# Query and key norms from an exponential of a logarithm and a Newton step, with another order of the first query tiles

## Chip, cores and metric

The kernel runs on one core of a Trainium2 chip. The metric is the device time of one execution in microseconds, the median over several runs. The profile is one further execution, taken by the hardware profiler, with times from the span's start.

## What is computed

One step of a hybrid decoder layer on a prompt of 1024 positions and 8 sample tokens: a recurrent branch (RG-LRU), three groups of dilated window attention with 8 heads of width 64 each, a gated merge and a SwiGLU feed-forward block. The change touches the normalisation of queries and keys alone:

```python
def rmsnorm(x, g):
    xf = x.astype(jnp.float32)
    y = xf * lax.rsqrt(jnp.mean(xf * xf, axis=-1, keepdims=True) + EPS)
    return (y * g.astype(jnp.float32)).astype(x.dtype)

q = rmsnorm(q.reshape(B, T, N_ATT_HEADS, HEAD_DIM), q_gain)
k = rmsnorm(k.reshape(B, T, N_ATT_HEADS, HEAD_DIM), k_gain)
```

## The kernel before, in words

The activations lie transposed: channels on the 128 partitions, 1032 positions along the row. Every projection runs through one list of weights (`stream`, lines 159 to 173), as units of 128 output channels (`unit`, lines 461 to 475). A unit is three parts of 344 columns; each part is 24 products of TensorE: 8 blocks of the inner dimension times three, because each float32 factor is split into a high and a low float32r half. SP loads the raw weights (line 329), GpSimd splits them by a cast (line 448) and a subtraction (line 450) as soon as the unit two places ahead has set the slot free, and two PSUM slots of three banks (`ups`) take the units in turn.

The stage here is `qk`: 24 units, i from 0 to 11, slot j = 0 and 1. Tile (i, j) is number 2i + j: the first 12 tiles are queries, the last 12 keys, each with two heads. What happens to a tile:

- ScalarE, `evac` (lines 988 to 997): copies the unit out of PSUM to `tmp(j)`, squares it to `tmp(2 + j)`, and rounds the square to a high half `sq_parts[0]`. The same two halves serve all tiles, so the third step waits until the sums of the tile before are done.
- VectorE, `square_low` (line 1270): the low half `sq_parts[1]`.
- TensorE, `stats` (lines 553 to 560): four products with a matrix of ones per head put the sum of squares, spread over the partitions of its head, in `aux` (two PSUM banks). They wait for the low half and until the tile before has been read out of `aux`. Their place is written out by hand: the sums of one tile stand between the second and the third part of the next unit (`qk`, lines 562 to 566); the first tiles have an order of their own (lines 570 to 583).
- ScalarE, `root` (line 1006): the square root of the mean plus epsilon, from `aux` to `tmp(4 + j)`.
- VectorE, `normed_qk` (lines 1332 to 1338): the reciprocal in place (line 1335), then the tile times gain times reciprocal to `tmp(6 + j)` (line 1337). This sets `tmp(j)` free for the next copy.
- ScalarE's queue, `store` (line 1001): the tile to DRAM, from where the attention loads it again.

Each engine runs its instructions in program order. VectorE's order in the loop is `normed_qk(i, 0)`, `square_low(i, 1)`, `normed_qk(i, 1)`, `square_low(i + 1, 0)`; ScalarE's is `root(i - 1, 1)`, `evac(i, 0)`, `store`, `root(i, 0)`, `evac(i, 1)`, `store`. Ahead of the loop stands the end of the recurrent branch: VectorE finishes its last block (`recur`, lines 1272 to 1290, with the low half of tile (0, 0) between its steps), while TensorE already works on units (0, 0), (0, 1) and (1, 0). Behind it stands the first pair of attention heads (`pair`, lines 591 to 653): 24 products of the next projection, the sums of the last tile, further products, the transposes of the values (line 614), the scores (line 625). SP's loads for it (lines 391 to 403) take the buffers of the stage over: the values go to `tmp(2)`, the bias to the row of `sq_parts[0]`.

A list of semaphores carries all this: `qsh_done` and `qsl_done` (halves of the square), `st_done` (sums), `rt_done` (root), `qn_done` (normed tile), `qn_stored` (stored). `z_done` counts the blocks of the recurrent branch after line 1286, `lru_done` those after line 1289.

Of the kernel before, what the change touches and what calls it, by code (L numbers as in the profile page):

```python
# [23 lines left out]
ALU = mybir.AluOpType  # L24
ACT = mybir.ActivationFunctionType
# [3 lines left out]
P = 128  # L29
D = 1024  # L30
SEQ = 1024
# [4 lines left out]
KT = D // P  # L36
HD = 64
# [7 lines left out]
EPS = 1e-6  # L45
# [47 lines left out]
def build(nc, A, O):  # L93

    with ExitStack() as ctx:
# [12 lines left out]
        big1 = sb("big1", [P, 2, KT, NT], F32R)  # L108
# [35 lines left out]
        def tmp(n):  # L144

            return x1[:, n, :]
# [33 lines left out]
        def two(name):  # L180

            return [sem(f"{name}{j}") for j in range(2)]
# [23 lines left out]
        out_done, lru_done = sem("out_done"), sem("lru_done")  # L206

        qsq_done, st_done, rt_done, qn_done = two("qsq_done"), two("st_done"), two("rt_done"), two("qn_done")
        qsh_done, qsl_done = two("qsh_done"), two("qsl_done")
        qn_stored = two("qn_stored")  # L210
        sqc_done = sem("sqc_done")
# [110 lines left out]
        def _(sp):  # L322
            for name, iters, nk, src, f0, f1, step, k0 in stream:
# [67 lines left out]
                if name == "att0":  # L391
                    first = 1
                    weights(0, 0)
                    weights(0, 1)
                    for n in range(4):
                        sp.wait_ge(v_stored[n], 16)
                    sp.wait_ge(qn_stored[0], 16 * 8)
                    query_loads(0, 0)
                    sp.wait_ge(qsl_done[0], 12)
                    value_load(0, 0)  # L400
                    sp.wait_ge(bt_fill, 16)
                    sp.wait_ge(st_done[1], 13)
                    bias_load(0, 0)
# [56 lines left out]
        def _(pe):  # L460
# [92 lines left out]
            def stats(j, i):  # L553

                pe.wait_ge(qsl_done[j], i + 1)
                pe.wait_ge(rt_done[1 - j], i + 1)
                for c in range(2):
                    for a in range(2):
                        ins = nc.tensor.matmul(aux[:, c, :], bones_r[:], sq_parts[a][:, c * 512:(c + 1) * 512], start=(a == 0), stop=(a == 1))  # L559
                ins.then_inc(st_done[j], 1)  # L560
# [5 lines left out]
                    unit("qk", i, j, big1, parts=(2,))  # L566

            pe.sem_inc(rt_done[1], 1)
            pe.sem_inc(st_done[1], 1)
            for c in range(2):  # L570
                unit("qk", 0, 0, big1, parts=(c,))
# [4 lines left out]
            unit("qk", 1, 0, big1, parts=(0,))  # L576
            stats(0, 0)
            unit("qk", 1, 0, big1, parts=(1, 2))
            unit("qk", 1, 1, big1, parts=(0,))
            stats(1, 0)  # L580
            unit("qk", 1, 1, big1, parts=(1,))
            stats(0, 1)
            unit("qk", 1, 1, big1, parts=(2,))
            with pe.Fori(2, 12) as i:
# [5 lines left out]
            for g in range(NG):  # L590
                def pair(i, first, marks):
# [14 lines left out]
                    if first:  # L606
                        stats(1, 11)
                        pieces(8, marks[0])
                        pe.wait_ge(ps_free[1], T0["att0"] + 1)
                        pe.wait_ge(rt_done[1], 13)  # L610
                    pe.wait_ge(v_ld, i * 16 + 16 * (4 * g + 1))
                    pe.wait_ge(pt_ev, i * 4 + (16 * g + 1))
                    for b in range(8):
# [214 lines left out]
        def _(act):  # L828
# [174 lines left out]
            def root(i, j):  # L1003
                act.wait_ge(st_done[j], i + (1 + j))
                act.wait_ge(qn_done[j], i + 1)
                nc.scalar.activation(tmp(4 + j)[:, 0:SEQ], aux[:].rearrange("p b n -> p (b n)"), ACT.Sqrt, scale=1.0 / HD, bias=epst[:])\  # L1006
                    .then_inc(rt_done[j], 1)

            act.wait_ge(u_done, KT + 1)
            evac(0, 0)  # L1010
            act.wait_ge(lru_done, KT)
            act.dma_start(O["lru_out"], sout[:]).then_inc(out_done, 16)
            act.dma_start(O["state_out"], stc[:]).then_inc(out_done, 16)
            root(0, 0)
            evac(0, 1)
            with act.Fori(1, 12) as i:
                root(i - 1, 1)
                evac(i, 0)
# [177 lines left out]
        def _(dve):  # L1196
# [111 lines left out]
            normed(7)  # L1308
            normed_low(6)
            normed_low(7)  # L1310
            nc.vector.tensor_copy(bones_r[:], bones[:])
            for c in range(2):
                nc.vector.tensor_copy(gqk[:, 6 * c:6 * c + 6], gq2[:, c:c + 1].broadcast_to([P, 6]))
            step.step(nc.vector.tensor_scalar(bmrg[:], bmrg[:], 0.5, None, ALU.mult))
            dve.wait_ge(unit_done[1], T0["lru"] + 2)
            nc.vector.tensor_tensor(chunks(GE), ups_v[1], chunks(rinv), ALU.mult).then_inc(ps_free[1], 1)
# [13 lines left out]


            def normed_qk(i, j):
                rms_t = tmp(4 + j)[:, 0:SEQ]
                dve.wait_ge(rt_done[j], i + (1 + j))
                step.step(nc.vector.reciprocal(rms_t, rms_t))  # L1335
                dve.wait_ge(qn_stored[j], i * 16 + 16)
                nc.vector.scalar_tensor_tensor(tmp(6 + j)[:, 0:SEQ], tmp(j)[:, 0:SEQ], gqk[:, ds(i, 1)],
                                               rms_t, ALU.mult, ALU.mult).then_inc(qn_done[j], 1)

            with dve.Fori(0, 11) as i:  # L1340
                step.loop(i, 2)
                normed_qk(i, 0)
                square_low(i, 1)
                normed_qk(i, 1)
                square_low(i + 1, 0)
            step.end(11)
            step.loop(11, 2, 11)
            normed_qk(11, 0)
            square_low(11, 1)
            normed_qk(11, 1)  # L1350
# [40 lines left out]
            def s_norm():  # L1391
# [4 lines left out]
                step.step(nc.vector.reciprocal(rms, rms))  # L1396
                for c in range(2):
                    own = sqkv[:, 12 * c:12 * c + 12, :].rearrange("p f b -> p (f b)")
                    step.step(nc.vector.scalar_tensor_tensor(own, own, gqk[:, 6 * c:6 * c + 1], rms[:, 96 * c:96 * c + 96], ALU.mult, ALU.mult))
                dve.sem_inc(sq_normed, 1)  # L1400

            def s_build():
# [268 lines left out]
```

## Time and profile before

| What | Value |
|---|---|
| median of 3 runs | 2072.24 us (2071.32 to 2073.37) |
| the profiled execution | 2071.17 us |
| its span, first to last instruction | 2069.4 us |
| mean granted clock of TensorE | 0.993 |
| busy: TensorE, VectorE, ScalarE, GpSimd | 97%, 44%, 25%, 27% of the span |
| VectorE's reciprocals of line 1335 | 24, 157.3 us |

The span is the profiled execution without what lies before its first and after its last instruction. Engines are named in the rows by PE (TensorE's products; PEld its weight loads), DVE (VectorE), ACT (ScalarE), POOL (GpSimd) and SP; a queue that issues transfers has a q behind its engine. In a timeline a row is a start in us, a length in us, the engine, the source line, the operation, the tile written and those read, and how many instructions are merged; in brackets stands how long the engine was idle before it, and what ended that.

### The profile page before, as it was taken

What the parts mean: (1) busy time and instruction counts of PE and PEld (TensorE: products, weight loads), DVE (VectorE), ACT (ScalarE), POOL (GpSimd) and SP (SyncE); (2) the same over time, 40 slices, a digit from 0 to 9 for tenths busy, and PEclk for the clock granted to TensorE, in tenths of its full rate; (3) what the DMA queues carried; (4) which work ended last, traced back from release to release, by engine and by line L of the source; (5) the groups of instructions that cost most, each with busy time, mean ns of one, the idle gap of its engine ahead of it and who ended that gap; (6) DMA issues with size and microseconds to landing.
All of it is one profiled execution on the core that took longest, in us unless ns stands there. A gap on an engine that the chain in (4) does not pass through costs nothing.

```text
span 2069.4 us, 32282 instructions
## 1 busy us (share of the span) xinstructions
PE 2014.0 (97%) x12884; PEld 1952.3 (94%) x12884; DVE 905.9 (44%) x919; ACT 509.3 (25%) x726; POOL 552.1 (27%) x325
## 2 busy tenths in 40 slices
PE   7999998999989999999989899999999999999999
PEld 7999997999979999999978899999999999999999
DVE  6666677777762332222266553433311233212331
ACT  5366653333333433333311111201000000000000
POOL 2323332222211111111122143323323232323322
PEclk9999999999999999999999999999999999999999
DMA  5211111222223323334286361111111111111112
GB/s 200 97 44 43 43 46 61 93 90 81 101 97 135 116 97 136 114 111 149 87 307 236 125 239 51 44 48 51 41 51 41 51 42 49 51 41 51 41 59 84
DMA packets 71595, 188.45 MB, mean 91 GB/s; under 512 B 9313, under 2 KB 28796, under 8 KB 70780
## 3 DMA queue, kind: packets, MB, share of 16 engines
q1 hardware_dynamic: 41456, 136.97, 19.5%
q10 hardware_dynamic: 30092, 50.81, 6.7%
q8 instruction: 34, 0.56, 0.1%
q14 instruction: 13, 0.11, 0.0%
HBM read 145.09 MB, written 45.81 MB: 92 GB/s over the span
## 4 chain that ended last, share of the span: by engine, by line
PE 89%; DVE 6%; ACT 1%; issue 1%; DMA 1%; POOL 0%; ACTq 0%; SPq 0%; DVEq 0%; POOLq 0%
PE ups L472 64%; PE ups L600 13%; PE ups L625 3%; PE ups L650 3%; PE aux L637 2%; DVE x L1335 1%; PE aux L538 1%; PE aux L559 1%; PE ups L486 1%; PE aux L614 0%; DVE x L1489 0%; DVE x L1259 0%; DMA x<-o_s 0%; DVE x L1280 0%; ACT x L1076 0%
## 5 line engine op out<-in xcount | busy, mean ns | idle before, releaser
L472 PE MATMUL ups<-big,wsp 128*128 128x344 f32 x9216 | 1477.3, 321 | 9.1 <-POOL wsp L450 6.6
L472 PEld LDWEIGHTS ups<-big,wsp 128*128 128x128 f32 x9216 | 1459.4, 189 | 24.0 <-issue 16.9
L448 POOL CAST wsp<-wraw 128x1024 fp32r<-128x1024 f32 (+2 forms) x160 | 167.8, 1049 | 1485.0 <-issue 724.0
L450 POOL TENSOR_TENSOR wsp<-wraw,wsp 128x1024 fp32r<-128x1024 f32 (+2 forms) x160 | 384.0, 2400 | 12.8
L600 PE MATMUL ups<-big,wsp 128*128 128x344 f32 x1728 | 291.8, 324 | 0.0
L600 PEld LDWEIGHTS ups<-big,wsp 128*128 128x128 f32 x1728 | 272.7, 189 | 5.3 <-issue 5.2
L1335 DVE RECIPROCAL x<-x 128x1024 f32<-128x1024 f32 x24 | 157.3, 6553 | 74.4 <-ACT x L1006 74.4
L1372 DVE SCALAR_TENSOR_TENSOR x<-ups,ext 128x256 f32<-128x256 f32 (+1 forms) x96 | 48.0, 542 | 235.4 <-PE aux L637 147.4
L1181 ACT ACTIVATE ext<-ext 128x1032 f32<-128x1032 f32 x22 | 23.6, 1071 | 482.5 <-DVE ext L1589 482.4
L1591 DVE TENSOR_TENSOR ext<-ups,ext 128x1032 f32<-128x1032 f32 x22 | 27.1, 1233 | 215.4 <-PE ups L472 215.4
L1605 DVE TENSOR_TENSOR x<-ups,x 128x1032 f32 x24 | 29.6, 1233 | 203.6 <-PE ups L472 203.6
L1076 ACT ACTIVATE x<-x,ext 128x128 f32<-128x128 f32 (+1 forms) x192 | 71.2, 442 | 58.8 <-DVE ext L1380 58.4
L1594 DVE TENSOR_TENSOR ext<-ext 128x1032 f32<-128x1032 f32 x22 | 71.3, 3241 | 4.8 <-DVE ext L1591 4.8
L1589 DVE TENSOR_TENSOR ext<-ups,ext 128x1032 f32<-128x1032 f32 x22 | 27.1, 1234 | 105.3 <-PE ups L472 104.9
L625 PE MATMUL ups<-ext 64*128 64x128 f32 (+1 forms) x384 | 67.1, 476 | 4.7 <-DVEq L1357 4.7
L650 PE MATMUL ups<-x 128*128 128x65 f32 x560 | 67.8, 270 | 0.0
L650 PEld LDWEIGHTS ups<-x 128*128 128x128 f32 x560 | 66.8, 192 | 0.0
L1006 ACT ACTIVATE x<-aux,epst 128x1024 f32<-128x1024 f32 x24 | 26.8, 1117 | 132.5 <-PE aux L559 122.9
L625 PEld LDWEIGHTS ups<-ext 64*128 64x128 f32 x384 | 43.5, 281 | 14.6 <-issue 13.1
L1385 DVE COPY x<-ups 128x260 f32<-128x260 f32 x48 | 20.4, 425 | 81.4 <-PE ups L650 81.4
L1066 ACT ACTIVATE x<-aux 128x768 f32<-128x768 f32 (+1 forms) x32 | 28.6, 895 | 83.6 <-PE ups L650 67.5
L1378 DVE TENSOR_REDUCE x<-x 128x2 f32<-128x256 f32 (+1 forms) x96 | 47.6, 538 | 1.6
(190 smaller groups left out, 1147.9 us busy)
## 6 DMA issues: line engine op xcount, KB each, us to landing
wraw<-w_in SPq DMA_DIRECT2D x52, 512.0 KB, 3.4
wraw<-w_ffn_in SPq DMA_DIRECT2D x44, 512.0 KB, 3.2
out_qkv<-x ACTq DMA_DIRECT2D x28, 512.0 KB, 2.7
ext<-out_qkv SPq DMA_DIRECT2D x24, 512.0 KB, 4.3
x<-x_T SPq DMA_DIRECT2D x16, 516.0 KB, 8.2
x<-gate_s SPq DMA_DIRECT2D x16, 516.0 KB, 4.1
wraw<-w_merge SPq DMA_DIRECT2D x16, 512.0 KB, 4.9
wraw<-w_ffn_out SPq DMA_DIRECT2D x16, 512.0 KB, 3.5
```

Of the source, the lines that this page charges most:

```text
L448: nc.gpsimd.tensor_copy(hi, raw).then_inc(w_hi, 1)
L450: nc.gpsimd.tensor_tensor(lo, raw, hi.bitcast(F32), ALU.subtract).then_inc(w_split[slot], 1)
L472: ins = nc.tensor.matmul(ups[:, slot, c, 0:CH], wsp[:, slot, w, k, :], src[:, a, k, c * CH:(c + 1) * CH], start=(k == 0 and w + a == 0), s ...
L600: ins = nc.tensor.matmul(ups[:, 0, c, 0:CH], wsp[:, slot, w, k, :], big1[:, a2, k, c * CH:(c + 1) * CH], start=(k == 0 and w + a2 == 0), s ...
L625: ins = nc.tensor.matmul(s_bank[:, hh, 256 * m + 256 - P * nk:256 * m + 256], toks(QT, g, b)[hr], toks(KTT, g, b, nk)[hr], start=True, sto ...
L637: ins = nc.tensor.transpose(pt_bank[:, hh, c:c + P], SB[:, hh, c:c + P], ident[:])
L650: ins = nc.tensor.matmul(o_bank[:, at:at + HD + 1], PTS[:, hh, c:c + P], VTOK[:, b + 1 - nk + k, hh, :], start=(k == 0), stop=(k == nk - 1))
L1076: ins = nc.scalar.activation(SB[:, hh, cols], SB[:, hh, cols], ACT.Exp, bias=NM[:, 2 * m + hh:2 * m + hh + 1])
L1335: step.step(nc.vector.reciprocal(rms_t, rms_t))
L1372: ins = nc.vector.scalar_tensor_tensor(SB[:, :, cols], s_bank[:, :, cols], SCALE, BT[:, :, 0:P * nk][:, :, ::-1], ALU.mult, ALU.add)
L1378: ins = nc.vector.tensor_reduce(OT[:, 2 * n + m, :, HD + 1], SB[:, :, cols], AX_X, ALU.max)
L1594: step.step(nc.vector.tensor_tensor(ext[:, 1, 0:NT], ext[:, 0, 0:NT], ext[:, 1, 0:NT], ALU.mult))
```

## The change

ScalarE's root becomes two operations: the logarithm of the sum of squares plus epsilon, and the exponential of minus half of it, an estimate y of the reciprocal root. VectorE's reciprocal becomes a Newton step of three products: t = (sum + epsilon) y, t = t y, t = (t - 3) y, which with a gain of minus one half is the corrected value. The mean's 1/64 goes into the matrix of ones. The first product reads `aux` again, so `aux` is set free after it (a new semaphore `nt_done` takes the place of `rt_done` in TensorE's waits). The products use `tmp(2 + j)`, so SP's first load of values waits until tile (11, 0) is normed. At the stage's start ScalarE copies tile (0, 1) before the first root and issues two small output transfers after it; VectorE takes the low halves of (0, 1) and (1, 0) ahead of the tiles they stood behind; TensorE takes the sums of (0, 1) and (1, 0) at other places.

```diff
@@ -206 +206 @@
         qsq_done, st_done, rt_done, qn_done = two("qsq_done"), two("st_done"), two("rt_done"), two("qn_done")
+        lg_done, nt_done = two("lg_done"), two("nt_done")
@@ -396 +397 @@
                         sp.wait_ge(v_stored[n], 16)
                     sp.wait_ge(qn_stored[0], 16 * 8)
                     query_loads(0, 0)
-                    sp.wait_ge(qsl_done[0], 12)
+                    sp.wait_ge(qn_done[0], 13)
                     value_load(0, 0)
                     sp.wait_ge(bt_fill, 16)
                     sp.wait_ge(st_done[1], 13)
@@ -553 +554 @@
             def stats(j, i):
 
                 pe.wait_ge(qsl_done[j], i + 1)
-                pe.wait_ge(rt_done[1 - j], i + 1)
+                pe.wait_ge(nt_done[1 - j], i + 1)
                 for c in range(2):
                     for a in range(2):
                         ins = nc.tensor.matmul(aux[:, c, :], bones_r[:], sq_parts[a][:, c * 512:(c + 1) * 512], start=(a == 0), stop=(a == 1))
@@ -566 +567 @@
                     unit("qk", i, j, big1, parts=(2,))
 
             pe.sem_inc(rt_done[1], 1)
+            pe.sem_inc(nt_done[1], 1)
             pe.sem_inc(st_done[1], 1)
             for c in range(2):
                 unit("qk", 0, 0, big1, parts=(c,))
@@ -576 +578 @@
             unit("qk", 1, 0, big1, parts=(0,))
             stats(0, 0)
             unit("qk", 1, 0, big1, parts=(1, 2))
-            unit("qk", 1, 1, big1, parts=(0,))
             stats(1, 0)
-            unit("qk", 1, 1, big1, parts=(1,))
+            unit("qk", 1, 1, big1, parts=(0, 1))
             stats(0, 1)
             unit("qk", 1, 1, big1, parts=(2,))
             with pe.Fori(2, 12) as i:
@@ -607 +608 @@
                         stats(1, 11)
                         pieces(8, marks[0])
                         pe.wait_ge(ps_free[1], T0["att0"] + 1)
-                        pe.wait_ge(rt_done[1], 13)
+                        pe.wait_ge(nt_done[1], 13)
                     pe.wait_ge(v_ld, i * 16 + 16 * (4 * g + 1))
                     pe.wait_ge(pt_ev, i * 4 + (16 * g + 1))
                     for b in range(8):
@@ -1003 +1004 @@
             def root(i, j):
                 act.wait_ge(st_done[j], i + (1 + j))
                 act.wait_ge(qn_done[j], i + 1)
-                nc.scalar.activation(tmp(4 + j)[:, 0:SEQ], aux[:].rearrange("p b n -> p (b n)"), ACT.Sqrt, scale=1.0 / HD, bias=epst[:])\
+                nc.scalar.activation(tmp(4 + j)[:, 0:SEQ], aux[:].rearrange("p b n -> p (b n)"), ACT.Ln, bias=epst[:]).then_inc(lg_done[j], 1)
+                act.wait_ge(lg_done[j], i + 1)
+                nc.scalar.activation(tmp(4 + j)[:, 0:SEQ], tmp(4 + j)[:, 0:SEQ], ACT.Exp, scale=-0.5)\
                     .then_inc(rt_done[j], 1)
 
             act.wait_ge(u_done, KT + 1)
             evac(0, 0)
+            act.wait_ge(z_done, KT + 1)
+            evac(0, 1)
             act.wait_ge(lru_done, KT)
+            root(0, 0)
             act.dma_start(O["lru_out"], sout[:]).then_inc(out_done, 16)
             act.dma_start(O["state_out"], stc[:]).then_inc(out_done, 16)
-            root(0, 0)
-            evac(0, 1)
             with act.Fori(1, 12) as i:
                 root(i - 1, 1)
                 evac(i, 0)
@@ -1308 +1312 @@
             normed(7)
             normed_low(6)
             normed_low(7)
-            nc.vector.tensor_copy(bones_r[:], bones[:])
+            nc.vector.tensor_scalar(bones_r[:], bones[:], 1.0 / HD, None, ALU.mult)
             for c in range(2):
-                nc.vector.tensor_copy(gqk[:, 6 * c:6 * c + 6], gq2[:, c:c + 1].broadcast_to([P, 6]))
+                nc.vector.tensor_scalar(gqk[:, 6 * c:6 * c + 6], gq2[:, c:c + 1].broadcast_to([P, 6]), -0.5, None, ALU.mult)
             step.step(nc.vector.tensor_scalar(bmrg[:], bmrg[:], 0.5, None, ALU.mult))
             dve.wait_ge(unit_done[1], T0["lru"] + 2)
             nc.vector.tensor_tensor(chunks(GE), ups_v[1], chunks(rinv), ALU.mult).then_inc(ps_free[1], 1)
@@ -1330 +1334 @@
 
 
             def normed_qk(i, j):
-                rms_t = tmp(4 + j)[:, 0:SEQ]
+                y, t = tmp(4 + j)[:, 0:SEQ], tmp(2 + j)[:, 0:SEQ]
                 dve.wait_ge(rt_done[j], i + (1 + j))
-                step.step(nc.vector.reciprocal(rms_t, rms_t))
+                step.step(nc.vector.scalar_tensor_tensor(t, aux[:].rearrange("p b n -> p (b n)"), EPS, y, ALU.add, ALU.mult))
+                dve.sem_inc(nt_done[j], 1)
+                step.step(nc.vector.tensor_tensor(t, t, y, ALU.mult))
+                step.step(nc.vector.scalar_tensor_tensor(t, t, -3.0, y, ALU.add, ALU.mult))
                 dve.wait_ge(qn_stored[j], i * 16 + 16)
                 nc.vector.scalar_tensor_tensor(tmp(6 + j)[:, 0:SEQ], tmp(j)[:, 0:SEQ], gqk[:, ds(i, 1)],
-                                               rms_t, ALU.mult, ALU.mult).then_inc(qn_done[j], 1)
-
-            with dve.Fori(0, 11) as i:
-                step.loop(i, 2)
+                                               t, ALU.mult, ALU.mult).then_inc(qn_done[j], 1)
+
+            square_low(0, 1)
+            normed_qk(0, 0)
+            square_low(1, 0)
+            normed_qk(0, 1)
+            with dve.Fori(1, 11) as i:
+                step.loop(i, 6, 1)
                 normed_qk(i, 0)
                 square_low(i, 1)
                 normed_qk(i, 1)
                 square_low(i + 1, 0)
-            step.end(11)
-            step.loop(11, 2, 11)
+            step.end(10)
+            step.loop(11, 6, 11)
             normed_qk(11, 0)
             square_low(11, 1)
             normed_qk(11, 1)
@@ -1396 +1407 @@
                 step.step(nc.vector.reciprocal(rms, rms))
                 for c in range(2):
                     own = sqkv[:, 12 * c:12 * c + 12, :].rearrange("p f b -> p (f b)")
-                    step.step(nc.vector.scalar_tensor_tensor(own, own, gqk[:, 6 * c:6 * c + 1], rms[:, 96 * c:96 * c + 96], ALU.mult, ALU.mult))
+                    step.step(nc.vector.scalar_tensor_tensor(own, own, gq2[:, c:c + 1], rms[:, 96 * c:96 * c + 96], ALU.mult, ALU.mult))
                 dve.sem_inc(sq_normed, 1)
 
             def s_build():
```

## Rows read from the trace of the kernel before

**Rows 1.** The page, busy time: us, share of the span, instructions.

```profile
PE 2014.0 (97%) x12884; PEld 1952.3 (94%) x12884; DVE 905.9 (44%) x919; ACT 509.3 (25%) x726; POOL 552.1 (27%) x325
```

**Rows 2.** Busy time by stage: stretch, length, engines, then granted clock.

```profile
core 0: us, PE busy (x) PEld busy (x) DVE busy (x) ACT busy (x) POOL busy (x), PEclk, DMA share, GB/s
255.00:342.40 87.40, 77.92 (x462) 75.01 (x461) 62.11 (x43) 42.23 (x47) 23.53 (x12) 0.96 0.15 52
342.40:575.34 232.94, 232.94 (x1446) 229.55 (x1446) 170.50 (x57) 83.12 (x95) 65.47 (x38) 1.00 0.25 88
```

**Rows 3.** TensorE's timeline, 300 to 345 us.

```profile
302.04 11.49 PE L472 MATMUL ups<-big,wsp 128*128 128x344 f32 x72
316.54 1.20 PE L559 MATMUL aux<-ext_r,bones_r 128*128 128x512 f32 x4 [3.01 <-DVE ext_r L1270]
...
327.98 2.07 PE L559 MATMUL aux<-ext_r,bones_r 128*128 128x512 f32 x4 [6.48 <-DVE ext_r L1270]
...
342.40 1.09 PE L559 MATMUL aux<-ext_r,bones_r 128*128 128x512 f32 x4
```

**Rows 4.** Timeline of all engines in the loop, 425 to 442 us.

```profile
428.21 1.09 PE L559 MATMUL aux<-ext_r,bones_r 128*128 128x512 f32 x4
...
429.35 1.12 ACT L1006 ACTIVATE x<-aux,epst 128x1024 f32<-128x1024 f32 x1 [5.16 <-PE aux L559]
430.49 6.55 DVE L1335 RECIPROCAL x<-x 128x1024 f32<-128x1024 f32 x1 [3.25 <-ACT x L1006]
433.12 1.03 ACT L991 ACTIVATE x<-ups 128x1032 f32<-128x1032 f32 x1 [2.66 <-PE ups L472]
433.25 1.04 POOL L448 CAST wsp<-wraw 128x1024 fp32r<-128x1024 f32 x1 [8.72 <-issue]
...
434.37 2.40 POOL L450 TENSOR_TENSOR wsp<-wraw,wsp 128x1024 fp32r<-128x1024 f32 x1
...
437.27 1.28 DVE L1337 SCALAR_TENSOR_TENSOR x<-x,gqk 128x1024 f32<-128x1024 f32 x1 [0.23 <-DVE x L1335]
438.48 1.22 DVE L1270 TENSOR_TENSOR ext_r<-x,ext_r 128x1024 fp32r<-128x1024 f32 x1
```

**Rows 5.** Timeline of all engines ahead of the loop, 297 to 300 us.

```profile
297.66 2.01 POOL L448 CAST wsp<-wraw 128x1024 fp32r<-128x1024 f32 x1 [7.80 <-issue]
298.69 2.07 DVE L1286 TENSOR_TENSOR x<-x 128x1032 f32<-128x1032 f32 x1
299.75 3.26 POOL L450 TENSOR_TENSOR wsp<-wraw,wsp 128x1024 fp32r<-128x1024 f32 x1
```

**Rows 6.** Two lines of the feed-forward block: shortest, median, longest in ns.

```profile
L1594 DVE TENSOR_TENSOR ext<-ext x22: 2515/3276/3281, 1340.8 to 1998.1; 128x1032 f32<-128x1032 f32 x22
...
L1591 DVE TENSOR_TENSOR ext<-ups,ext x22: 1233/1233/1234, 1339.4 to 1996.7; 128x1032 f32<-128x1032 f32 x22
```

**Rows 7.** ScalarE's timeline: table loads before and in the stage.

```profile
2.14 1.28 ACT L852 ACT_TABLE_LOAD   x1 [2.14 <-issue]
...
30.44 0.21 ACT L869 ACTIVATE sqkv<-sqkv 128x8 f32<-128x8 f32 x1 [1.30 <-issue]
30.67 1.28 ACT L871 ACT_TABLE_LOAD   x1
...
288.90 1.28 ACT L949 ACT_TABLE_LOAD   x1
...
292.24 1.07 ACT L949 ACTIVATE x<-x 128x1032 f32<-128x1032 f32 x1 [2.06 <-DVE x L1275]
```

**Rows 8.** Timeline of all engines, 303 to 307 us.

```profile
303.59 1.23 DVE L1289 TENSOR_TENSOR big<-x,big 128x1032 fp32r<-128x1032 f32 x1
...
306.12 1.12 ACT L1006 ACTIVATE x<-aux,epst 128x1024 f32<-128x1024 f32 x1 [9.60 <-issue]
```

**Rows 9.** TensorE's timeline at the end of the stage, 580 to 600 us.

```profile
586.68 1.20 PE L559 MATMUL aux<-ext_r,bones_r 128*128 128x512 f32 x4 [2.69 <-DVE ext_r L1270]
...
597.23 1.66 PE L625 MATMUL ups<-ext 64*128 64x128 f32 x8 [4.71 <-DVEq L1357]
```

**Rows 10.** The page, transfers: issues, KB each, us to landing.

```profile
ext<-out_qkv SPq DMA_DIRECT2D x24, 512.0 KB, 4.3
```

## The prediction

> **What bounds it now.** I read the page first: TensorE is busy 97% of the span [rows 1], so the change can pay only where TensorE stands still, and can cost wherever it makes TensorE stand. The table of stages comes next [rows 2]: in the 87.40 us up to the loop's first sums TensorE is busy 77.92 us at a granted clock of 0.96; in the 232.94 us of the loop it is busy all the time. The first stage has something to win, the loop has only something to lose. TensorE's timeline [rows 3] then shows what there is to win: it stands 3.01 us before the sums of tile (0, 1) and 6.48 us before those of (1, 0), each time for VectorE's low part of a square. The four products behind the second stand take 2.07 us where others take 1.09: the clock fell while the engine stood.
>
> The loop's timeline [rows 4] gives the cycle of one tile. I count from the start of its sums, s (428.21 here). The loop's stage, from the sums of (1, 1) to those of (11, 0), holds 19 intervals, so they are 232.94 / 19 = 12.26 us long. The root starts at s + 1.14 and takes 1.12; the reciprocal takes 6.55, the scaling 1.28, the next tile's low part 1.22 and ends at 439.70, 0.77 before TensorE wants it (440.47). So a tile may come 0.7 us later on VectorE before the loop pays. GpSimd's split of weights runs at s + 5.04 for 1.04 and s + 6.16 for 2.40, wholly beside the reciprocal.
>
> **The change, part by part.**
>
> *The reciprocal goes* (6.55), three products come (1.22 to 1.28 each by the scaling and the low part [rows 4], some 3.7 together), and each waits for the one before: between nothing and the 0.23 that stands before the scaling; I take 0.1 to 0.2. Alone that would shorten VectorE's part by about 2.5.
>
> *The products meet GpSimd.* A VectorE operation with two operands in SBUF did not run beside the weight split: at 297.66 the cast took 2.01 for 1.04 behind a VectorE operation, then the product of line 1286 took 2.07, ending 1.09 after the cast, then the subtraction took 3.26 for 2.40 [rows 5]. Line 1594, both operands in SBUF, takes 3276 ns in the median; line 1591, one operand in PSUM, takes 1233 in all 22 cases [rows 6]. The reciprocal, with one operand, met nothing. Of the new products the first reads PSUM and passes; the second, the third and the scaling have two SBUF operands and fall just where the split runs. A waiter that gets in ends about 1.09 (VectorE) or 2.25 (the subtraction) after the holder.
>
> *One ScalarE operation becomes two.* Both are near the 1.12 of the root and the 1.03 of the copy [rows 4]; I take 1.12 and 1.07. Whether tables must be loaded between them is the open point. Only one place shows the two functions together [rows 7]: the exponential of line 869 ran under the table loaded for line 852, and the logarithm of line 871 right behind it needed a load of 1.28. So the table then in place held the one and not the other, and functions seem to be served one at a time, not by a table that suits the whole stretch. The Trainium skill says that one set has both functions, so that a logarithm and an exponential cost one load ("ScalarE: Activation LUTs", Table sets: the hidden batching unit), and that loads are placed by the longest run ("ScalarE activation tables: per-element evaluation and per-set limits", Table sets in the compiler and the runtime); by these the loop would have no load, and the sum would be that of the first rival. The load at line 871 speaks against the longest run. From [rows 7] I take two loads per tile: one before the logarithm, which is hidden, since a load ran ahead of its operation's wait at line 949 (288.90, operation at 292.24 [rows 7]), and one of 1.28 between the two, on the path. Ends: no load, and both on the path.
>
> *The loop with two loads.* A stand costs TensorE's sums some 0.1 more (1.20 for 1.09 [rows 3]), so the logarithm runs from s + 1.23 to 2.35, the load to 3.65, the exponential to 4.73, the first product to 5.98. The cast starts at 5.13 and ends at 6.17; the second product, ready at 6.13, ends at 7.26; the subtraction, waiting, ends at 9.51; the third product at 10.6, the scaling at 11.93, the low part at 13.07. The sums follow at 13.12 instead of 12.26: 19 x 0.86 = 16.3 us lost. ScalarE's three copies, from about s + 5.0 to 8.4, are hidden beneath. Gaps hardly count here, since the cast's end sets the second product: without the stand's 0.1 the period is 13.0 (14 lost). But if that product comes 0.1 later it finds the subtraction ahead of it (6.25 to 8.65) and the period is 13.5 (23.6 lost).
>
> *The new order of the first tiles.* Now ScalarE's copies of (0, 1) start once line 1286 is done (300.76 [rows 5]), not after the root at 306.12 with its 9.60 us of waiting [rows 8]; they end at 304.1 and VectorE takes the low part at 304.9, right behind line 1289 (303.59 + 1.23). The two small output transfers that stood ahead of the root on ScalarE's queue are issued behind it; nothing waits for them before the end. The root's pair with a load ends at 309.05, the first product at 310.3; that product now, not ScalarE, gives `aux` free, and TensorE, ready at 309.6 (302.04 and 48 of the 72 products of 11.49 us [rows 3]), waits for it until 310.4. The split takes the lock at 309.95 (GpSimd follows the tile's end by some 0.35 [rows 4]), so the products and the scaling of (0, 0) end only at 316.75; the copies of (1, 0) wait for that and end at 320.0, the low part at 321.25, the first product of (0, 1), which stands behind the low part on VectorE, at 322.4. The sums of (1, 0) start at 322.5 (TensorE ready at 319.0) instead of 327.98; the next ones by the loop's steps at 335.65 instead of 342.40. Gain 6.75.
>
> *The end of the stage.* Only 24 products stand before the last sums; they start at s + 11.34 now (586.68, after 2.69 us of standing [rows 9]). With the loop's steps they start at s + 13.12, 1.8 later; then 1.23 + 1.12 + 1.28 + 1.07 + 4 products of 5.2 against 1.23 + 1.12 + 6.55 + 1.28: 0.3 less. The attention's first scores (597.23 [rows 9]) come about 1.5 later. After that TensorE's work shifts as a whole.
>
> *Moved waits.* SP's value load now waits until the scaling of tile (11, 0) is done, since the products use that buffer. Behind it SP holds the bias load, which waits for the last sums anyway, and these come after that scaling; a load of this size lands 4.3 us later [rows 10], so at 591.6, before the transposes that need it (at 594.4, behind the last first product). Its cover is 2.8 us; what a later load took beyond that, TensorE would stand. TensorE's own wait there moves from the root to the first product, 594.4, when it is ready at 593.3: inside the wait for the scores. The scaled constants replace copies of the same shapes: nothing.
>
> Sum, against the profiled execution (2071.17; the median of the runs, 2072.24, is 1.07 above it): 2071.17 - 6.75 + 16.3 + 1.5 = **2082.2**. Its own range, from the two other periods: 2079 to 2090.
>
> **Rivals.**
>
> *One set serves both functions.* No load in the loop. For it: no row shows which table line 871 took, and one that holds both would serve all that follows; against it: at line 852 the choice fell on one that doesn't. This is what the Trainium skill's rule above would make of the loop. Exponential done at s + 3.5, first product at 4.8, second ahead of the cast (5.13) to 6.0, cast to 6.9, third to 8.0, subtraction to 10.3, scaling to 11.4, low part to 12.5: 12.60, so 19 x 0.34 = 6.5 lost, the start 7.75 won (334.65), the end 0.3 won: 2069.6. If the second product misses its turn before the cast, the period is 13.0 and the sum 2077.
>
> *The products run unhindered* (the other side): the lock of [rows 5] does not reach these operands, or falls between them. The price is the blocked time alone, and it decides from the point where the low part ends before s + 12.2. Then no interval is lost: with loads 2060.8 (start 9.95, end 0.4 won), without 2058.7 (start 9.9, end 2.6 won). Against it: all 22 cases of line 1594.
>
> *Both loads on the path*: 24 us more, 2107.
>
> **Chances.** Two loads 0.52, one set 0.35, unhindered 0.10, both on the path 0.03. About 0.2%, 4.1 us, is what a measurement can tell from no change. Faster: the unhindered 0.10 and a good quarter of the one-set case, where gaps of 0.15 less would save 3 us more (0.10): 0.20. Same: 0.20 of one set and 0.04 of the first: 0.24. Slower: the rest, 0.56. The range 2066 to 2090 holds the first two cases and leaves out the unhindered one, the last and the tails, together less than 0.2.
>
> **What would show it.** Right: table loads of 1283 ns before line 1006 and between its two operations; products of about 2.1 to 3.3 us median beside the split; sums 13.1 us apart; the loop's first sums near 335.6; TensorE waiting for line 1270 in every tile. No loads in the loop and sums 12.6 apart is the first rival; products at 1.22 throughout and sums 12.26 apart the second. What would make me wrong first is the table set, then the order in which the second product and the cast get in.

## The result and the profile after

The changed kernel takes 2091.24 us in the median of four runs (2090.01 to 2091.64), beside 2072.64 us (2071.32 to 2073.37) for the kernel before: a ratio of 1.009, with a 95% interval of 1.0076 to 1.0104. It is slower by about 0.9%. The forecast was 2082.2 us with a range from 2066 to 2090, so the measured time lies 1.2 us above the range. The direction and the mechanism came out, but three terms of the sum were off and a fourth loss had none, and each of the four makes the sum too short. The profiled execution took 2091.26 us (span 2089.5), 20.1 more than the one before (2071.17); the medians differ by 18.6, because the profiled execution before was 1.5 below the median of its runs.

The page of the kernel after, its sections on busy time (compare [rows 1]) and on the chain that ended last, and behind them that chain before:

```profile
PE 2024.0 (97%) x12884; PEld 1955.5 (94%) x12884; DVE 884.5 (42%) x967; ACT 590.8 (28%) x794; POOL 574.1 (27%) x325
PE 78%; DVE 13%; ACT 4%; issue 4%; DMA 1%; POOL 0%; DVEq 0%; SPq 0%; ACTq 0%; POOLq 0%
```

```profile
PE 89%; DVE 6%; ACT 1%; issue 1%; DMA 1%; POOL 0%; ACTq 0%; SPq 0%; DVEq 0%; POOLq 0%
```

TensorE still is busy 97% of the span, but VectorE and ScalarE now hold 17% of the chain where they held 7%. The stages show which stretch changed. The table of stages, from 46 us ahead of the first sums to the loop's first sums and from there to the end of the loop (columns as in [rows 2]):

```profile
258.50:340.70 82.20, 77.26 (x462) 74.15 (x460) 58.09 (x49) 54.56 (x57) 25.23 (x12) 0.98 0.15 55
340.70:593.45 252.75, 238.04 (x1444) 229.21 (x1444) 155.29 (x95) 151.97 (x152) 83.39 (x38) 1.00 0.21 81
```

The loop's 19 intervals take 252.75 us where they took 232.94 [rows 2], and TensorE is idle for 14.7 us of them. The loop's period is 252.75 / 19 = 13.30 us instead of 12.26. TensorE's waits over the whole kernel name the cause, VectorE's low part at the end of each tile (us in total, times, longest; line 1340 sets `aux` free after the first product):

```profile
PE aux L560 <- DVE ext_r L1274: 19.9, 21, 4.4
PE aux L560 <- DVEq L1340: 4.1, 2, 3.5
```

The table loads and VectorE's products, by source line (duration in ns: least, median, most; then first and last start):

```profile
L1007 ACT ACT_TABLE_LOAD  x24: 1283/1283/1283, 307.7 to 601.8; - x24
L1009 ACT ACT_TABLE_LOAD  x24: 1283/1283/1283, 310.1 to 609.9; - x24
L1339 DVE SCALAR_TENSOR_TENSOR x<-aux,x x24: 1217/1225/1226, 312.5 to 612.3; 128x1024 f32<-128x1024 f32 x24
L1342 DVE SCALAR_TENSOR_TENSOR x<-x x24: 1224/3302/3307, 315.6 to 614.9; 128x1024 f32<-128x1024 f32 x24
```

There are 48 loads, one before each logarithm and one before each exponential. The first product, which reads PSUM, always takes 1.22; the third takes 3.30 in the median. The second (line 1341 in the next rows) takes 1.23 in the median although both its operands lie in SBUF: in this tile it begins 0.04 before the cast ends. One tile of the loop, with the sums that follow (rows of other work left out; compare [rows 4]):

```profile
433.75 1.20 PE L560 MATMUL aux<-ext_r,bones_r 128*128 128x512 f32 x4 [0.68 <-DVE ext_r L1274]
...
434.99 1.12 ACT L1007 ACTIVATE x<-aux,epst 128x1024 f32<-128x1024 f32 x1 [4.81 <-PE aux L560]
436.12 1.28 ACT L1009 ACT_TABLE_LOAD   x1
437.42 1.06 ACT L1009 ACTIVATE x<-x 128x1024 f32<-128x1024 f32 x1
438.51 1.23 DVE L1339 SCALAR_TENSOR_TENSOR x<-aux,x 128x1024 f32<-128x1024 f32 x1 [4.81 <-ACT x L1009]
...
438.89 1.04 POOL L449 CAST wsp<-wraw 128x1024 fp32r<-128x1024 f32 x1 [8.73 <-issue]
...
439.89 1.23 DVE L1341 TENSOR_TENSOR x<-x 128x1024 f32<-128x1024 f32 x1 [0.15 <-DVE x L1339]
440.01 3.36 POOL L451 TENSOR_TENSOR wsp<-wraw,wsp 128x1024 fp32r<-128x1024 f32 x1
...
441.15 3.30 DVE L1342 SCALAR_TENSOR_TENSOR x<-x 128x1024 f32<-128x1024 f32 x1
...
442.11 1.28 ACT L1007 ACT_TABLE_LOAD   x1
444.69 1.29 DVE L1344 SCALAR_TENSOR_TENSOR x<-x,gqk 128x1024 f32<-128x1024 f32 x1 [0.24 <-DVE x L1342]
445.89 1.22 DVE L1274 TENSOR_TENSOR ext_r<-x,ext_r 128x1024 fp32r<-128x1024 f32 x1
...
447.17 1.20 PE L560 MATMUL aux<-ext_r,bones_r 128*128 128x512 f32 x4 [0.88 <-DVE ext_r L1274]
```

The logarithm's load (442.11) lies ahead of its wait and costs nothing; the exponential's (436.12) is on the path. The chain then is cast, second product, subtraction, third product: the subtraction ends 2.25 after the second product (441.12 to 443.37), the third product 1.08 after the subtraction (444.45).

The start and the end of the stage in TensorE's timeline (compare [rows 3, 9]):

```profile
304.60 1.09 PE L560 MATMUL aux<-ext_r,bones_r 128*128 128x512 f32 x4
...
326.09 2.05 PE L560 MATMUL aux<-ext_r,bones_r 128*128 128x512 f32 x4 [3.46 <-DVEq L1340]
...
340.70 1.20 PE L560 MATMUL aux<-ext_r,bones_r 128*128 128x512 f32 x4 [0.80 <-DVE ext_r L1274]
```

```profile
593.45 1.20 PE L560 MATMUL aux<-ext_r,bones_r 128*128 128x512 f32 x4 [0.68 <-DVE ext_r L1274]
...
606.64 2.08 PE L560 MATMUL aux<-ext_r,bones_r 128*128 128x512 f32 x4 [4.44 <-DVE ext_r L1274]
...
617.75 0.93 PE L626 MATMUL ups<-ext 64*128 64x128 f32 x8 [2.72 <-DVEq L1368]
```

From these marks, profile against profile: the first sums already come 3.5 us later (304.60 against 301.11); from there to the loop's first sums it takes 36.10 us instead of 41.29, so the start gains 5.2; the loop loses 252.75 - 232.94 = 19.8; from the last first sums of the loop to the first scores it takes 24.30 us instead of 21.89, a loss of 2.4; the rest of the kernel is 0.4 shorter. 3.5 - 5.2 + 19.8 + 2.4 - 0.4 = 20.1.

### The profile page after: what moved, and what is told of

Read it like the earlier page. It is cut to its first block, busy times and chain, and to the rows that moved or that the text cites. A ratio compares the mean times of both kernels' runs of the same rounds, so it can differ in the third digit from the quotient of the medians.

```text
span 2089.5 us, 32456 instructions
## 1 busy us (share of the span) xinstructions
PE 2024.0 (97%) x12884; PEld 1955.5 (94%) x12884; DVE 884.5 (42%) x967; ACT 590.8 (28%) x794; POOL 574.1 (27%) x325
## 4 chain that ended last, share of the span: by engine, by line
PE 78%; DVE 13%; ACT 4%; issue 4%; DMA 1%; POOL 0%; DVEq 0%; SPq 0%; ACTq 0%; POOLq 0%
PE ups L473 53%; PE ups L601 12%; DVE x L1342 4%; PE ups L626 3%; PE ups L651 3%; PE aux L638 2%; DVE x L1339 1%; DVE x L1341 1%; PE aux L560 1%; DVE ext_r L1274 1%; ACT x L1007 1%; ACT x L1009 1%; PE aux L539 1%; PE ups L487 1%; PE aux L615 0%
## 5 line engine op out<-in xcount | busy, mean ns | idle before, releaser
L451 POOL TENSOR_TENSOR wsp<-wraw,wsp 128x1024 fp32r<-128x1024 f32 (+2 forms) x160 | 406.6, 2541 | 12.8
L1342 DVE SCALAR_TENSOR_TENSOR x<-x 128x1024 f32<-128x1024 f32 x24 | 75.1, 3128 | 0.8
L1339 DVE SCALAR_TENSOR_TENSOR x<-aux,x 128x1024 f32<-128x1024 f32 x24 | 29.4, 1224 | 106.5 <-ACT x L1009 106.5
L560 PE MATMUL aux<-ext_r,bones_r 128*128 128x512 f32 x96 | 30.3, 440 | 24.1 <-DVE ext_r L1274 19.9
```

Of the source, the lines that this page charges most:

```text
L451: nc.gpsimd.tensor_tensor(lo, raw, hi.bitcast(F32), ALU.subtract).then_inc(w_split[slot], 1)
L1339: step.step(nc.vector.scalar_tensor_tensor(t, aux[:].rearrange("p b n -> p (b n)"), EPS, y, ALU.add, ALU.mult))
L1342: step.step(nc.vector.scalar_tensor_tensor(t, t, -3.0, y, ALU.add, ALU.mult))
```

## The experiments

Two theories stood against each other for the loop: the table load on the path (1.28 us per tile), and the turns that the products take with GpSimd's weight split. A third question was what the new order of the first tiles is worth by itself. "Period" below is a kernel's loop divided by its 19 intervals. Ratios are against the kernel before on the same chip (medians 2072.42 and 2073.39 us in the two sets of runs). The edits are shown shortened, against the changed kernel (the last one against the kernel with one table); "..." stands for what is left out.

**The order alone.** The changed kernel with the square root and the reciprocal back; the matrix of ones, the gains and SP's value load are those of before too.

```diff
-  activation(tmp(4 + j), aux, ACT.Ln, bias=epst) ; activation(tmp(4 + j), tmp(4 + j), ACT.Exp, scale=-0.5)
+  activation(tmp(4 + j), aux, ACT.Sqrt, scale=1.0 / HD, bias=epst)
-  scalar_tensor_tensor(t, aux, EPS, y, add, mult) ; tensor_tensor(t, t, y, mult) ; scalar_tensor_tensor(t, t, -3.0, y, add, mult)
+  reciprocal(rms_t, rms_t)
-  pe.wait_ge(nt_done[1 - j], i + 1)
+  pe.wait_ge(rt_done[1 - j], i + 1)
```

> The square root and the reciprocal of before with the new order of the first tiles alone. My theory (the loop pays for one table load and for products that take turns with the weight split; the order pays back some us once): no stand in the loop, sums 12.26 us apart, the loop's first sums near 335 instead of 342.4, time 2064 to 2067. Rival, the new order itself costs (a wait of ScalarE for the recurrent branch, low halves ahead of other work): time above 2075.

It took 2072.03 us, ratio 1.0001 [0.9991, 1.001]: no gain, and a miss. TensorE's and VectorE's timelines show why:

```profile
318.87 1.20 PE L560 MATMUL aux<-ext_r,bones_r 128*128 128x512 f32 x4 [0.92 <-DVE ext_r L1272]
...
337.79 2.07 PE L560 MATMUL aux<-ext_r,bones_r 128*128 128x512 f32 x4 [6.39 <-DVE ext_r L1272]
```

```profile
318.73 6.55 DVE L1337 RECIPROCAL x<-x 128x1024 f32<-128x1024 f32 x1
325.31 3.29 DVE L1339 SCALAR_TENSOR_TENSOR x<-x,gqk 128x1024 f32<-128x1024 f32 x1
328.53 6.54 DVE L1337 RECIPROCAL x<-x 128x1024 f32<-128x1024 f32 x1
```

The two stands of [rows 3] (3.01 and 6.48) shrink to 0.92, ahead of (1, 0), but one of 6.39 comes one tile later: two reciprocals stand one behind the other ahead of the low part of (1, 1), and the scaling between them takes 3.29 instead of 1.28, since it falls on GpSimd's subtraction (325.13 to 327.52). The order moves the stand as long as VectorE needs 6.55 us per tile. At the loop's first sums 4.3 us are won (36.96 us from the first sums to 337.79, against 41.29); the sums there again take 2.07, and the next ones come 14.29 later instead of 12.26. At the first scores 1.3 are left (294.83 against 296.12).

**The root alone.** The changed kernel with the old order of the first tiles on ScalarE, TensorE and VectorE.

```diff
             unit("qk", 1, 0, big1, parts=(1, 2))
+            unit("qk", 1, 1, big1, parts=(0,))
             stats(1, 0)
-            unit("qk", 1, 1, big1, parts=(0, 1))
+            unit("qk", 1, 1, big1, parts=(1,))
...
-            act.wait_ge(z_done, KT + 1)
-            evac(0, 1)
             act.wait_ge(lru_done, KT)
-            root(0, 0)
             act.dma_start(O["lru_out"], sout[:]).then_inc(out_done, 16)
             act.dma_start(O["state_out"], stc[:]).then_inc(out_done, 16)
+            root(0, 0)
+            evac(0, 1)
...
-            square_low(0, 1)
-            normed_qk(0, 0)
-            square_low(1, 0)
-            normed_qk(0, 1)
-            with dve.Fori(1, 11) as i:
+            with dve.Fori(0, 11) as i:
```

> The logarithm, exponential and products in the order of before. My theory: sums 13.3 us apart as in the changed kernel, first sums of the loop about where they were (342 to 344), so 2093 to 2097, some 5 us more than the changed kernel. Rival, the order costs: below 2086.

2096.07 us, ratio 1.0119 [1.0097, 1.0141], period 13.30, as expected. So the loop's loss is the root's. With the new root the order is worth about 5 us by the medians (2096.07 against 2091.24; the two intervals overlap a little) and 7.5 by the profiles, from the first sums to the first scores (320.69 against 313.15); with the old root it was 1.3 by the same marks. The two parts of the change help each other: the order pays only where the tiles come off VectorE fast enough.

**No loads.** The logarithm is replaced by a function that ScalarE runs under the exponential's table.

```diff
-                nc.scalar.activation(tmp(4 + j)[:, 0:SEQ], aux..., ACT.Ln, bias=epst[:])
+                nc.scalar.activation(tmp(4 + j)[:, 0:SEQ], aux..., ACT.Tanh, bias=epst[:])
```

> The changed kernel with a hyperbolic tangent in place of the logarithm, a function that shares a table with the exponential; the root is left out, the operations and their lengths stay. My theory (load and turns each cost): no load in the loop, the second product gets in ahead of the cast, sums 12.6 us apart, time 2070 to 2075. Rival one, the loads are all of it: 12.26 us apart, time 2062 to 2066. Rival two, the turns with the weight split are all of it: still 13.2 to 13.4 apart, time 2086 to 2091.

2070.0 us, ratio 0.9991 [0.9981, 1.0], period 12.58. Against the changed kernel 21 us come back. Profile against profile 13.8 of them lie in the loop (19 x 0.72), 2.9 in the start and 1.6 in the end; the other 3.1 lie ahead of the first sums, where the edit changes nothing (see "Ahead of the stage" below). The loop still is longer than before, and its rows show the turns alone:

```profile
427.54 1.23 DVE L1341 TENSOR_TENSOR x<-x 128x1024 f32<-128x1024 f32 x1 [0.15 <-DVE x L1339]
...
427.83 1.84 POOL L449 CAST wsp<-wraw 128x1024 fp32r<-128x1024 f32 x1 [7.41 <-issue]
...
428.80 1.94 DVE L1342 SCALAR_TENSOR_TENSOR x<-x 128x1024 f32<-128x1024 f32 x1
429.75 3.24 POOL L451 TENSOR_TENSOR wsp<-wraw,wsp 128x1024 fp32r<-128x1024 f32 x1
...
430.98 3.10 DVE L1344 SCALAR_TENSOR_TENSOR x<-x,gqk 128x1024 f32<-128x1024 f32 x1 [0.24 <-DVE x L1342]
```

The second product now is ahead of the cast, the third takes its turn before the subtraction, and the scaling is the one that stands behind it. Two operations still wait, but the one behind the subtraction is the last.

**No turns, loads kept.** The second and the third product read the sums in PSUM instead of the product before them, so each has one operand in SBUF.

```diff
+                step.step(nc.vector.tensor_tensor(t, aux..., y, ALU.mult))
+                step.step(nc.vector.scalar_tensor_tensor(t, aux..., -3.0, y, ALU.add, ALU.mult))
                 dve.sem_inc(nt_done[j], 1)
-                step.step(nc.vector.tensor_tensor(t, t, y, ALU.mult))
-                step.step(nc.vector.scalar_tensor_tensor(t, t, -3.0, y, ALU.add, ALU.mult))
```

> The changed kernel with the second and third product reading the sums in PSUM in place of the product before, so that each has one operand in SBUF; the Newton step is left out, the loads stay, and the sums' banks are set free after the third product. My theory: the two products take 1.22 us beside the weight split, the low half ends about 11.2 us after the sums' start, sums 12.26 apart with all loads in place; the start loses some 3 us by the later release; time 2066 to 2073. Rival one, the loads are all of it: sums still above 13 apart, time 2088 or more. Rival two, the turns are all of it: 12.26 apart as well.

2069.96 us, ratio 0.9988 [0.9977, 0.9998], period 12.26. One tile of its loop:

```profile
430.19 1.28 ACT L1009 ACT_TABLE_LOAD   x1
...
433.83 1.23 DVE L1340 TENSOR_TENSOR x<-aux,x 128x1024 f32<-128x1024 f32 x1
...
434.07 2.41 POOL L451 TENSOR_TENSOR wsp<-wraw,wsp 128x1024 fp32r<-128x1024 f32 x1
...
435.09 1.22 DVE L1341 SCALAR_TENSOR_TENSOR x<-aux,x 128x1024 f32<-128x1024 f32 x1
...
437.86 1.22 DVE L1274 TENSOR_TENSOR ext_r<-x,ext_r 128x1024 fp32r<-128x1024 f32 x1
440.18 1.09 PE L560 MATMUL aux<-ext_r,bones_r 128*128 128x512 f32 x4
```

The load still is there, on the same path, and costs nothing in the loop: products and subtraction run side by side (1.22 and 2.41), the low part is done at 439.08, 1.1 us before TensorE wants it.

**Neither.** Both edits.

> Both taken away: the hyperbolic tangent in place of the logarithm, so no load, and the second and third product reading PSUM; the root and the Newton step are left out. My theory (the loop loses only where load and turns together use up its slack): sums 12.26 us apart, as with either the turns removed; the start some 3 to 5 us earlier than with the loads; time 2062 to 2068. Rival, something else in the change holds the loop (the steps of VectorE, the release of the sums' banks after a product): above 12.4 us apart.

2065.17 us, ratio 0.9956 [0.9941, 0.997], period 12.26. The four cells together, as period in us:

| | products take turns | products read PSUM |
|---|---|---|
| two loads per tile | 13.30 | 12.26 |
| no load | 12.58 | 12.26 |

Both theories hold, but not as two costs that add up. Without the turns a tile has 1.1 us to spare even with the load in it; with the turns it is 0.32 short without any load, and the load then costs 0.72 more. That is less than the load's 1.28, because without the load the split comes later: its cast waits for the second product, and the subtraction ends 10.30 us after the sums' start (432.99, sums at 422.69) instead of 9.62 (443.37, sums at 433.75). Outside the loop the load is not free without the turns either: in the start, from the first sums to the loop's first, the kernel with it takes 37.92 us and the one without 34.79.

**One table.** Does the loop need the loads at all? One explicit load of a table that holds both functions is put ahead of the first root; nothing else is changed.

```diff
             evac(0, 1)
+            nc.scalar.add_instruction(mybir.InstLoadActFuncSet(act_func_set_id=6, ...))
             act.wait_ge(lru_done, KT)
             root(0, 0)
```

> The changed kernel, all its arithmetic in place, with one table load written out ahead of the first root, of a table that holds both functions. My theory: no further load in the stage, sums 12.58 us apart as with the tangent, the loop's first sums at 334 to 335 (or 3.5 later where the clock falls at the program's start), time 2068 to 2072, so within 0.2% of the kernel before. Rival, the loads are placed again per operation: 13.3 apart, 2090. Rival, the loads were all of it: 12.26 apart, 2062 to 2066.

2071.12 us, ratio 0.9986 [0.9977, 0.9994], period 12.57; by source line the stage has this one load left:

```profile
L1016 ACT ACT_TABLE_LOAD  x1: 1283/1283/1283, 304.5 to 304.5; - x1
```

From the first sums to the first scores this kernel takes 295.76 us, the changed one 313.15: 17.4 us of the change's cost were a choice of tables, not the arithmetic. The Trainium skill ("ScalarE: Activation LUTs", Table sets: the hidden batching unit) says that a logarithm and an exponential share one set and cost one load. This run agrees with it, and the changed kernel shows that it doesn't come by itself: without the explicit load each of the 24 pairs had two, 48 in all.

**One product on ScalarE.** On top of that, the square of the estimate is taken by ScalarE, so that VectorE has two products in place of three; all the arithmetic stays.

```diff
...
+                act.wait_ge(ex_done[j], i + 1)
+                nc.scalar.activation(tmp(2 + j)[:, 0:SEQ], tmp(4 + j)[:, 0:SEQ], ACT.Square).then_inc(rt_done[j], 1)
...
-                step.step(nc.vector.scalar_tensor_tensor(t, aux..., EPS, y, ALU.add, ALU.mult))
+                step.step(nc.vector.scalar_tensor_tensor(t, aux..., EPS, t, ALU.add, ALU.mult))
                 dve.sem_inc(nt_done[j], 1)
-                step.step(nc.vector.tensor_tensor(t, t, y, ALU.mult))
                 step.step(nc.vector.scalar_tensor_tensor(t, t, -3.0, y, ALU.add, ALU.mult))
```

> As the one before, and the square of the estimate is taken by ScalarE, so that VectorE's Newton step is two products, of which the first reads PSUM; all arithmetic in place. My theory: the one product left that takes turns ends about 7.3 us after the sums' start, the scaling 10.6, the low half 11.75, inside the 12.26, so no stand in the loop; time 2060 to 2066. Rival, ScalarE's third operation makes it late (it runs into its copies of the next tile) or the turns still cost: sums 12.5 or more apart, 2070 or more.

2066.25 us, ratio 0.9955 [0.9942, 0.9968], period 12.26: faster than both kernels, by some 7 us than before and 25 than the changed one; the time is 0.25 above the range expected, the period as expected. Its loop:

```profile
426.56 1.22 DVE L1341 SCALAR_TENSOR_TENSOR x<-aux,x 128x1024 f32<-128x1024 f32 x1 [5.08 <-ACT x L1011]
...
427.14 1.04 POOL L449 CAST wsp<-wraw 128x1024 fp32r<-128x1024 f32 x1 [7.87 <-issue]
427.94 1.31 DVE L1343 SCALAR_TENSOR_TENSOR x<-x 128x1024 f32<-128x1024 f32 x1 [0.15 <-DVE x L1341]
...
429.48 3.12 DVE L1345 SCALAR_TENSOR_TENSOR x<-x,gqk 128x1024 f32<-128x1024 f32 x1 [0.23 <-DVE x L1343]
...
432.53 1.21 DVE L1276 TENSOR_TENSOR ext_r<-x,ext_r 128x1024 fp32r<-128x1024 f32 x1
434.36 1.09 PE L560 MATMUL aux<-ext_r,bones_r 128*128 128x512 f32 x4
```

The cast falls beside the product that reads PSUM and has 0.24 left when the next one comes (427.94, cast to 428.18); only the scaling waits for the subtraction, and the low part is done at 433.74, 0.6 before TensorE wants it. In the start TensorE stands 0.49 and 2.32 us, and not at all at the loop's first sums. In the whole stage it waits for the low part once, for 3.0 us, at the last sums.

## Where the prediction was right, and where it was wrong

Profile against profile the change costs 20.1 us where the sum had 11.0. The path held; what failed is the size of three of its terms, the loop, the start and the end, and a fourth loss for which it had no term.

**The mechanism** was the predicted one. The loads are where it put them, one hidden, one of 1283 ns on the path; the first product passes; TensorE waits for the low part in every tile of the loop. The two causes were told apart by the four cells above.

**The loop's period** was forecast at 13.12 and is 13.30: 19.8 us lost, not 16.3. The step that failed is "Gaps hardly count here, since the cast's end sets the second product". By the tile above (sums at 433.75), that product was ready at 6.14 after the sums, as forecast (6.13), and the cast ended at 6.18. The forecast let the product end 1.09 after the cast, at 7.26; but it came only 0.04 before the cast's end, took its whole length (1.23) and ended at 7.37. Everything behind it moved by that 0.11. It came 0.12 ahead of the subtraction (440.01); that the order of the two held, and with it the period of 13.1 rather than the 13.5 of the prediction's other case, was in part luck. And the gap before the scaling does count, since nothing covers it: 0.24 in this tile, where the forecast had 0.05 (10.6 to 11.93 for an operation of 1.28). The neighbouring tile has 0.04 there, in the same view:

```profile
427.94 3.30 DVE L1342 SCALAR_TENSOR_TENSOR x<-x 128x1024 f32<-128x1024 f32 x1
...
431.28 1.28 DVE L1344 SCALAR_TENSOR_TENSOR x<-x,gqk 128x1024 f32<-128x1024 f32 x1
```

The intervals alternate accordingly: 13.42 for the tile above (433.75 to 447.17), 13.20 for the loop's last (580.25 to 593.45). The mean gap of 0.14 is 0.09 above the forecast's; with the 0.11 that makes up the 0.18 of the period to within 0.02.

**The start** was forecast to gain 6.75 and gains 5.2. Up to the sums of (1, 0) the steps held: 326.09, less the 3.5 us that this execution was late from the front, is 322.6, forecast 322.5. What the forecast left out is the clock. It counted the stand there at its own length (3.5, measured 3.46); behind it the sums took 2.05 us instead of 1.16, and the granted clock was 0.50, the lower of the engine's two levels (1.2 of 2.4 GHz). In the table of stages the granted clock is the third column from the end:

```profile
326.00:328.50 2.50, 2.41 (x6) 2.07 (x7) 2.42 (x2) 0.32 (x1) 0.00 (x0) 0.50 0.00 0
...
606.70:609.00 2.30, 2.30 (x6) 1.92 (x7) 0.00 (x0) 0.24 (x1) 0.00 (x0) 0.50 0.56 203
```

The next sums so came 14.61 later, not 13.15. The slower sums are 0.85 of that; besides, the cast of the weights, which waits until TensorE has set its slot free, came 6.42 after the sums' start instead of 5.14 as in the loop's tile, and the subtraction and the third product behind it:

```profile
332.51 1.04 POOL L449 CAST wsp<-wraw 128x1024 fp32r<-128x1024 f32 x1 [14.73 <-issue]
```

The row that should have told of the clock was cited: the clock had fallen behind the 6.48 us stand of [rows 3].

**The end** was forecast to lose 1.5 and loses 2.4, by the same step: the last sums came at 13.19 after the ones before (forecast 13.12), after a stand of 4.44 us, and took 2.08 us at a clock of 0.50, the second row above.

**Ahead of the stage** the forecast had no term at all, and 3.5 us are lost there. The table of stages over the kernel's first microseconds, before and after in turn:

```profile
10.00:26.00 16.00, 14.34 (x68) 12.44 (x69) 15.13 (x11) 12.44 (x13) 4.29 (x2) 1.00 0.65 243
```

```profile
10.00:26.00 16.00, 13.75 (x47) 10.84 (x48) 14.43 (x11) 11.79 (x13) 4.29 (x2) 0.79 0.68 260
```

The granted clock is 0.79 there instead of 1.00; 0.21 of 16 us is about 3.4 (0.35 of the 3.5 is there already when TensorE's first product starts, at 10.48 against 10.13). The code of this stretch is the same in all these kernels, and the kernel with one table, which differs from the changed one by a single instruction much later, has 1.00; the one with products from PSUM has 0.79 too, "Neither" and the last experiment have 0.89 each. So no edit of the change is shown to cause it, and the cause stays open. The kernel before is not free of a varying clock either: 25 of its runs took 2070.41 to 2077.81 us at mean granted clocks of 0.989 to 0.993, and its profiled execution, at 0.993, is among the least disturbed. That the timed runs of the changed kernel have this loss is likely but only argued: the profiled execution is one of the four, which lie within 1.7 us of each other, and the profiles of the changed kernel and of the one with one table differ by 17.4 us from the first sums to the first scores, their medians by 20.1.

Without the front's 3.5 the sum would have been short by 5.6: 3.5 in the loop, 1.6 in the start, 0.9 in the end, less 0.4 elsewhere. That would be 2087.8 us, inside the range; it took the front as well to leave it.

**The rivals.** That one set serves both functions did not happen in the changed kernel, but its numbers came true once the loads were gone: forecast period 12.60 and 2069.6 us, measured 12.57 and 2071.12 with one table, 12.58 and 2070.0 without the logarithm. Of the two statements of the Trainium skill that the prediction cites, the one on the joint set is borne out by the run with one table; the placement by the longest run is not what happened here, with 48 loads, and the row at line 871 [rows 7] had told that rightly. Unhindered products fall by the 3302 ns of the third product; the run that made them so shows that the point given for them (low part before 12.2) was the right one: at 11.16 after its sums (439.08 - 427.92) the period stays at 12.26. Both loads on the path did not happen either.

**The moved waits** cost nothing that the trace shows: the scores wait for VectorE, as before.

## What to carry to other kernels

Count an engine's saving only in the stretch where someone waits for it, and then count whom its replacement meets: here the products that replaced 6.55 us took 5.94 (438.51 to 444.45) and not the 3.7 of their lengths alone, because GpSimd worked at the same time. When two functions alternate on ScalarE, look for a table load between them and load a table that holds both by hand. When two delays share some slack, price them together: the load that cost nothing with the turns gone cost 0.72 us per tile on top of them.

## What was not expected of the hardware

- TensorE's clock fell to 0.50 behind stands of 3.46 and 4.44 us, and the sums behind them took 2.05 and 2.08 us instead of 1.16 to 1.20, so that such a stand costs more than its own length. The length of a single stand doesn't tell whether it happens: behind the 3.01 us of [rows 3] the clock was 1.00 (316.60 to 320.00), and behind 3.29 in the kernel without loads too (322 to 330), while behind the 2.32 us in the last experiment the unit's 72 products took 13.03 instead of 11.49, with a clock of 0.50 from 323.7 on.
- The clock fell near 18 us in some kernels' profiled executions and not in others, with the same code up to there (0.79, 0.89 and 1.00 over the same 16 us).
- VectorE's gap before the scaling is 0.24 and 0.04 in turn from tile to tile. The trace of the changed kernel lists ten register operations of VectorE's queue at the scaling's line (46 ns each, 338.1 to 577.7), and ten scalings that began behind the longer gap (2.4 us in all); in the tiles looked at, the register operation stands in the one with the longer gap (444.6, scaling at 444.69) and not in its neighbours. Whether it makes the gap was not tried.
